# A decoder trunk on one core: squares summed by VectorE, the first expert's rows found by themselves, output weights in order of use

## What is computed

```python
for l in range(DEPTH):
    h = rms_norm(x, mix_norm[l])
    p = h @ w_in[l]
    y = concat([rwkv7_mix(p), short_conv_mix(p), dilated_attention_mix(p)])
    x = x + y @ w_o[l]
    h = rms_norm(x, ffn_norm[l])
    if l == 0: x = x + swiglu(h, dense_wg, dense_wu, dense_wd)
    else:
        topv, topi = top_k(h @ router, 2); gates = softmax(topv)
        x = x + sum of gates * swiglu(h, moe_wg[e], moe_wu[e], moe_wd[e]) over the chosen e
```

## Time and profile before

| | us |
|---|---|
| median of 3 runs | 1449.14 |
| the profiled execution, whole | 1449.35 |
| its span, first to last instruction | 1447.5 |
| mean granted TensorE clock | 0.992 of full speed |
| TensorE busy | 1424.3 (98%) |
| weight load busy | 1100.1 (76%) |
| VectorE busy | 870.2 (60%) |
| ScalarE busy | 722.9 (50%) |
| GpSimd busy | 72.5 (5%) |
| transfers | 440.84 MB, mean 305 GB/s |

### The profile page before, as it was taken

The page is one execution under the profiler, slowest core; times in us unless marked ns, Lnnn a source line. Parts: engine busy times, 40 slices in busy tenths (PEclk is TensorE's granted clock), DMA queues, the critical chain, the costliest instruction groups (busy, mean ns, idle before and its releaser), DMA issues.

```text
span 1447.5 us, 24888 instructions
## 1 busy us (share of the span) xinstructions
PE 1424.3 (98%) x10480; PEld 1100.1 (76%) x10480; DVE 870.2 (60%) x1136; ACT 722.9 (50%) x991; POOL 72.5 (5%) x61
## 2 busy tenths in 40 slices
PE   8999999999999999999999999999999999999997
PEld 8988999999999889733788634888535888888532
DVE  7587855555557887311899311999203999899300
ACT  6545544444455645200888302888103887888200
POOL 0004000010000050000000000000000000000000
PEclk9999999999999999899999999999999999999999
DMA  9600455554544400999999999999999999999996
GB/s 342 221 36 4 186 193 185 193 176 175 175 163 175 139 3 3 392 416 421 421 420 422 421 422 421 421 421 420 421 421 422 420 414 423 407 421 415 348 422 263
DMA packets 64838, 440.84 MB, mean 305 GB/s; under 512 B 8000, under 2 KB 10576, under 8 KB 12112
## 3 DMA queue, kind: packets, MB, share of 16 engines
q1 hardware_dynamic: 63344, 434.46, 74.4%
q0 software_dynamic: 960, 3.15, 1.4%
q10 hardware_dynamic: 416, 1.57, 0.3%
HBM read 434.96 MB, written 2.62 MB: 302 GB/s over the span
## 4 chain that ended last, share of the span: by engine, by line
PE 91%; DMA 5%; DVE 2%; ACT 1%; issue 0%; SPq 0%; POOL 0%; DVEq 0%; POOLq 0%; ACTq 0%
PE bank L893 20%; PE bank L895 19%; PE bank L894 19%; PE bank L874 12%; PE bank L1605 11%; PE bank L1623 5%; DMA arena<-in_moe_wu 5%; PE bank L1568 1%; PE bank L1613 1%; PE bank L1638 1%; DMA ring<-in_w_in 0%; PE bank L1067 0%; PE bank L914 0%; PE bank L1320 0%; PE bank L1642 0%
## 5 line engine op out<-in xcount | busy, mean ns | idle before, releaser
L1744 ACT ACTIVATE w_hi<-ring 128x1024 fp32r<-128x1024 f32 x284 | 298.7, 1060 | 175.1 <-PE bank L895 169.4
L893 PE MATMUL bank<-w_hi,acts_hi 128*128 128x512 f32 x672 | 265.1, 394 | 0.0
L895 PE MATMUL bank<-w_hi,acts_lo 128*128 128x512 f32 x672 | 261.8, 390 | 0.0
L894 PE MATMUL bank<-w_lo,acts_hi 128*128 128x512 f32 x672 | 261.7, 389 | 0.0
L893 PE MATMUL bank<-acts_hi,w_hi 128*128 128x256 f32 x796 | 227.2, 285 | 1.1 <-DVE acts_lo L2497 0.8
L894 PE MATMUL bank<-acts_lo,w_hi 128*128 128x256 f32 x796 | 225.2, 283 | 0.0
L895 PE MATMUL bank<-acts_hi,w_lo 128*128 128x256 f32 x796 | 225.2, 283 | 0.0
L2568 DVE TENSOR_TENSOR w_lo<-arena,w_hi 128x1024 fp32r<-128x1024 f32 x144 | 175.1, 1224 | 13.2 <-ACT w_hi L1744 7.4
L2568 DVE TENSOR_TENSOR w_lo<-ring,w_hi 128x1024 fp32r<-128x1024 f32 x144 | 174.7, 1224 | 13.5 <-ACT w_hi L1744 7.7
L2903 DVE TENSOR_TENSOR arena<-arena,bank 128x256 f32<-128x256 f32 x28 | 11.8, 422 | 271.2 <-ACT arena L2171 271.2
L1744 ACT ACTIVATE w_hi<-arena 128x1024 fp32r<-128x1024 f32 x144 | 152.8, 1065 | 37.2 <-PE bank L895 37.2
(11 more groups left out here) (309 smaller groups left out, 1935.8 us busy)
## 6 DMA issues: line engine op xcount, KB each, us to landing
ring<-in_moe_wu SPq DMA_DIRECT2D x56, 1024.0 KB, 22.0
ring<-in_moe_wg SPq DMA_DIRECT2D x56, 1024.0 KB, 22.0
arena<-in_moe_wd SPq DMA_DIRECT2D x56, 1024.0 KB, 23.3
arena<-in_moe_wu SPq DMA_DIRECT2D x52, 1024.0 KB, 22.2
arena<-in_moe_wg SPq DMA_DIRECT2D x36, 1024.0 KB, 22.1
ring<-in_moe_wd SPq DMA_DIRECT2D x32, 1024.0 KB, 20.3
ring<-in_w_in SPq DMA_DIRECT2D x24, 1024.0 KB, 7.1
late<-in_moe_wg SPq DMA_DIRECT2D x16, 1024.0 KB, 22.8
```

The lines of the kernel that those rows point to most:

```text
L893: pe.matmul(out_, a_hi, b_hi, start=first, stop=False, **kw)
L894: pe.matmul(out_, a_hi, b_lo, start=False, stop=False, **kw)
L895: return pe.matmul(out_, a_lo, b_hi, start=False, stop=final, **kw)
L1744: return act.activation(o, i, ACT.Copy, **kw)
```

## The change

- **Sums of squares.** VectorE adds the eight squared slices up in `hT` with four instructions (`add_squares`: three of 128x512, one of 128x256) ahead of its next weight splits. TensorE then multiplies only the sum, with two products of one column in place of sixteen. This is done for n = 1 and n = 2.
- **The first expert's rows.** Who belongs to expert 0 is found without the full routing: a token does if fewer than two logits exceed its own for expert 0. Three rank products follow, then the seats. The raw rows `x_tok`, not the normalised ones, are gathered by four products of 512 columns, and the seats' inverse roots by four of one column; ScalarE scales the rows, TensorE turns them, and VectorE multiplies by the gains into `xb`. The full routing and the normalised rows come after that on VectorE, and the full ranks on TensorE behind the first half of the first chunk. The products of `keep_awake` are five, one before and two, two, two, one after. ScalarE waits for the normalised rows before it copies the first chunk (both use `spare`).
- **Output weights.** `w_o` is laid out on the host in the order of use, so its pieces 0 to 3 come from the halves in places 0 and 1. The expert weights' ring order becomes `late`, 0, 1, 4, 5, 2, 3 and the rest, and each load waits for the last user of its own place.

```diff
-            for two in (1, 2, 3, 0):
-                seen = max(WO_ORDER.index(2 * two), WO_ORDER.index(2 * two + 1)) + 1
-                stream += [("o", l, two, 0, (lo_ready, WO0[l] + seen))]
+            stream += [("o", l, two, 0, (lo_ready, WO0[l] + 2 * two + 2)) for two in range(KT // 2)]
...
         LATE = DEEP - 2
-        ring_places = [LATE] + e_slot[:SLOTS] + [s for s in range(SLOTS, DEEP) if s != LATE]
+        SPLIT_EARLY = (0, 1)
+        ring_places = [LATE, *SPLIT_EARLY] + [s for s in e_slot[:SLOTS] if s not in SPLIT_EARLY]
+        ring_places += [s for s in range(SLOTS, DEEP) if s != LATE]
...
-                            sp.wait_ge(*stream[e_before[n - 1]][4])
+                            sp.wait_ge(*stream[user[p_slot[n]]][4])
...
-            def sum_squares(n, k):
-
-                pe.wait_ge(sq_ready, KT * (n - 1) + k + 1)
+            def sum_squares(n):
+                pe.wait_ge(sums_stepped, 4 * n)
                 for b in range(2):
-                    last = pe.matmul(bank[SUM_BANKS[n]][:, b:b + 1], hT[:, k, b * P:(b + 1) * P], ones[:, 0:1],
-                                     start=k == b == 0, stop=k == KT - 1, skip_group_check=True)
-                if k == KT - 1:
-                    last.then_inc(ss_ready, 1)
+                    last = pe.matmul(bank[SUM_BANKS[n]][:, b:b + 1], hT[:, 0, b * P:(b + 1) * P], ones[:, 0:1],
+                                     start=b == 0, stop=True, skip_group_check=True)
+                last.then_inc(ss_ready, 1)
...
-                    elif j >= 2:
-                        sum_squares(1, 2 * j - 4)
-                        sum_squares(1, 2 * j - 3)
                 if l:
                     turn_rows(3)
-                    keep_awake(7, 5)
+                    keep_awake(7, 2)
...
                             if kind == "g" and j == 0 and q == 1:
-                                for k in range(4, KT):
-                                    sum_squares(1, k)
+                                sum_squares(1)
...
-            sel = small[:, 0:16]
-            pe.wait_ge(route_sel, 1)
-            mm(bank[6][:, 0:8], const("tri"), sel[:, 0:8])
-            mm(bank[6][:, 8:16], const("tri"), sel[:, 8:16], True, False)
-            mm(bank[6][:, 8:16], ones, sel[:, 0:8], False, True)
-            mm(bank[6][:, 16:24], ones, sel[:, 0:8], True, False)
-            mm(bank[6][:, 16:24], ones, sel[:, 8:16], False, True).then_inc(rank_done, 1)
-            keep_awake(7, 1)
+            def first_ranks():
+                pe.wait_ge(route_sel, 1)
+                mm(bank[5][:, 0:1], const("tri"), first_sel[:, 0:1])
+                mm(bank[5][:, 1:2], const("tri"), first_sel[:, 1:2], True, False)
+                mm(bank[5][:, 1:2], ones, first_sel[:, 0:1], False, True).then_inc(rank_done, 1)
+            def gather_first():
+                pe.wait_ge(hot_ready, 1)
+                pe.wait_ge(act_turned, 4)
+                for b in range(2):
+                    for g in range(2):
+                        last_ = pe.matmul(bank[1][g * C:(g + 1) * C, :], hot[0][:, b, 0:C],
+                                          x_tok[:, b, g * CW:(g + 1) * CW], start=b == 0, stop=b == 1,
+                                          skip_group_check=True)
+                pe.wait_ge(ms_ready, 4)
+                for b in range(2):
+                    for g in range(2):
+                        last_ = pe.matmul(bank[5][g * C:(g + 1) * C, 2:3], hot[0][:, b, 0:C], rms[:, b:b + 1],
+                                          start=b == 0, stop=b == 1, skip_group_check=True)
+                last_.then_inc(ga_done, 1)
+                keep_awake(7, 2)
+                pe.wait_ge(rows_kept, 1)
+                for i in range(4):
+                    last_ = pe.transpose(bank[2][:, i * P:(i + 1) * P], first_rows[:, i * P:(i + 1) * P], ident)
+                last_.then_inc(rows_kept, 1)
+                keep_awake(7, 1)
+            def all_ranks():
+                sel = small[:, 0:16]
+                pe.wait_ge(route_sel, 2)
+                mm(bank[5][:, 8:16], const("tri"), sel[:, 0:8])
+                mm(bank[5][:, 16:24], const("tri"), sel[:, 8:16], True, False)
+                mm(bank[5][:, 16:24], ones, sel[:, 0:8], False, True)
+                mm(bank[5][:, 24:32], ones, sel[:, 0:8], True, False)
+                mm(bank[5][:, 24:32], ones, sel[:, 8:16], False, True).then_inc(rank_done, 1)
...
-            gather_half(1, hot[0], True)
+            first_ranks()
+            keep_awake(7, 2)
+            gather_first()
...
+                        if q == hf == 0:
+                            all_ranks()
...
+            def keep_first_rows():
+                act.wait_ge(ga_done, 1)
+                act.wait_ge(seat_ready, 1)
+                act.activation(first_rows, bank[1][:, :], ACT.Identity, scale=seat_rms).then_inc(rows_kept, 1)
...
-            begin(0)
+            act.wait_ge(ht_ready, 2)
...
+            def add_squares(n, i):
+                dve.wait_ge(sq_ready, KT * (n - 1) + min(2 * i + 2, KT))
+                if i > 1:
+                    dve.wait_ge(sums_stepped, 4 * (n - 1) + i - 1)
+                if i < KT // 2:
+                    TT(hT[:, 0:2, :], hT[:, 0:2, :], hT[:, 2 * i:2 * i + 2, :], ALU.add).then_inc(sums_stepped, 1)
+                else:
+                    TT(hT[:, 0, :], hT[:, 0, :], hT[:, 1, :], ALU.add).then_inc(sums_stepped, 1)
...
+                add_squares(2, 1)
                 dve.wait_ge(x_ffn, 4)
                 for k in (KT - 2, KT - 1):
                     scaled_low(k, u_hi, u_lo, k, param(1, "mix_norm", k), u_high, KT, u_low)
+                for i in range(2, 5):
+                    add_squares(2, i)
...
+                    add_squares(1, 1)
                     for k in (KT - 2, KT - 1):
                         scaled_low(k, h_hi, h_lo, DENSE_PLACE[k], param(0, "ffn_norm", k), h_high, KT, h_low)
+                    for i in range(2, 5):
+                        add_squares(1, i)
...
-            largest(top1, first)
-            then(STT(logits, first, -3e38, logits, ALU.mult, ALU.add))
-            largest(top2, second)
-            TT(sel, first, second, ALU.add).then_inc(route_sel, 1)
-            dve.wait_ge(row_squared, 4)
-            TT(rms, row_sums[:, 0:2], row_sums[:, 2:4], ALU.add).then_inc(ss_ready, 1)
-            then(TT(e2, top2, top1, ALU.subtract))
-            dve.wait_ge(rt_ready, 4)
-            then(dve.reciprocal(rms, rms))
-            TT(e2, e2, rms, ALU.mult).then_inc(route_act, 1)
+            def first_members():
+                then(TT(per(cand), per(logits), stretch(per(logits)[:, :, 0], NE), ALU.is_gt))
+                then(dve.tensor_reduce(at_, per(cand), AX.X, ALU.add))
+                TS(first_sel, at_, 1.5, None, ALU.is_lt).then_inc(route_sel, 1)
+            def first_places():
+                dve.wait_ge(rank_done, 1)
+                then(STT(rank_first, bank[5][:, 0:2], 1.0, first_sel, ALU.add, ALU.mult))
+                STT(hot[0][:, :, 0:C], spread(const("iota")[:, 0:C], 2), 1.0, stretch(rank_first, C), ALU.add,
+                    ALU.is_equal).then_inc(hot_ready, 1)
+            def first_tokens():
+                dve.wait_ge(rows_kept, 2)
+                gains_of = prm[:, N_PARAM * (L - 1) + PARAM_COLS["ffn_norm"][0]:][:, 0:KT]
+                TT(xb.rearrange("p (g i) t -> p i g t", g=2),
+                   bank[2][:, :].rearrange("p (i g t) -> p i g t", i=4, g=2),
+                   gains_of.rearrange("p (g i o) -> p i g o", g=2, o=1).to_broadcast([P, 4, 2, C]),
+                   ALU.mult).then_inc(ga_kept, 1)
...
+            first_members()
+            dve.wait_ge(sums_stepped, 8 + 4)
+            TT(rms, row_sums[:, 0:2], row_sums[:, 2:4], ALU.add).then_inc(ss_ready, 1)
+            first_places()
+            dve.wait_ge(rt_ready, 4)
+            dve.reciprocal(rms, rms).then_inc(ms_ready, 1)
+            largest(top1, first)
+            dve.wait_ge(ga_done, 1)
+            dve.tensor_copy(seat_rms, bank[5][:, 2:3]).then_inc(seat_ready, 1)
+            then(STT(logits, first, -3e38, logits, ALU.mult, ALU.add))
+            first_tokens()
+            largest(top2, second)
+            TT(sel, first, second, ALU.add).then_inc(route_sel, 1)
+            then(TT(e2, top2, top1, ALU.subtract))
+            TT(e2, e2, rms, ALU.mult).then_inc(route_act, 1)
             dve.wait_ge(gain_in, 16)
             normal_rows(0)
-            dve.wait_ge(rank_done, 1)
-            then(STT(rank_first, per(bank[6][:, 0:16])[:, :, 0], 1.0, per(sel)[:, :, 0], ALU.add, ALU.mult))
-            STT(hot[0][:, :, 0:C], spread(const("iota")[:, 0:C], 2), 1.0, stretch(rank_first, C), ALU.add,
-                ALU.is_equal).then_inc(hot_ready, 1)
-            TS(rank_sums, bank[6][:, 0:3 * NE], 1.0, None, ALU.mult)
             normal_rows(1)
```

(9 more changed lines are left out.)

25 lines of the change are left out of this document (14 added, 11 removed).

## The result

The changed kernel takes 1436.36 us (median of 4 runs, 1435.42 to 1437.15), the kernel before 1448.74 (median of 4). The ratio on record is 0.9909, with a 95% interval of 0.9895 to 0.9924: 12.4 us faster by the medians, 13.2 (11.0 to 15.2) by the ratio times 1449.14. The forecast was 11.15 us. In the profiled executions the whole went from 1449.35 to 1437.15 (12.2 us) and the span from 1447.5 to 1435.3.

The account below looks back on a forecast made before the run. The expert stage was taken as bound almost equally by weight transfers and TensorE. 1449.35 - 4.75 (norms) - 6.4 (expert stage) = 1438.2, against the median 1438.0; range 1436 to 1445.

Parts of the forecast that it names:

- part 1: Sums of squares in the two norms: 1.0 us won in layer 0, 3.75 in layer 1, 4.75 in all.
- part 3: First expert's rows, routing: TensorE's path 5.6 us earlier, full ranks later costing 1.1 us.
- part 2: Output weights in order of use: two halves fetched within the recurrence, 5.0 us of transfer moved out of the later stretch.
- The two bounds: Expert stage: TensorE and transfers bind almost equally; speeding up only one gains at most 1.4 us, so both must move.
- Rival C: Routing: clock falls earlier, or early halves are useless because TensorE alone is late; 1 to 1.5 us left, 1443.3; chance 0.10.
- The smaller of the two: Expert stage: TensorE's own way 7.0 us ahead, transfers 6.4; the smaller, 6.4, holds.
- D: Layer 1's norm: clock still falls, from the 0.9 us stall for the reciprocal; 1.7 us less, 1439.7; chance 0.08.
- H: Norms: VectorE's adds cost as much as was saved, and Rival C besides; about 1447.5, no visible change; chance 0.06.
- One sign that the forecast set itself: Either norm: the forecast is wrong if TensorE idles for VectorE longer than 0.9 us.
- The clock in the routing: New routing before the first expert: full clock assumed, narrowly, because wide products fill most of its 8 us.
- B: New routing: clock falls at about 602 as before; 4.0 us instead of 6.4, 1440.4; chance 0.20.
- F: TensorE at half clock from the logits on: stream 4.8 us later, layer 1's clock lost too; 1451; chance 0.05.

Follow-up runs that it names:

- e1: The changed kernel again, unaltered, beside the kernel before on the first chip: 1435.78 us, ratio 0.991.
- e12: The changed kernel again, unaltered, on the third chip: 1436.36 us, ratio 0.9915.
- e5: Changed kernel with VectorE's last three additions behind two weight splits and TensorE's sum and spread one piece later, both norms: 1434.81 us, ratio 0.9905.
- e11: Changed kernel with the last three additions behind two weight splits, run again beside the unaltered changed kernel on the third chip: 1434.72 us, ratio 0.9904.
- e2: Changed kernel with the sums of squares undone, TensorE again multiplying all eight squared slices: 1442.57 us, ratio 0.9959.
- e3: Changed kernel with the old ring order, so only one half is fetched early; w_o keeps its new layout: 1441.27 us, ratio 0.9949.
- e10: Kernel before with only the new first-expert routing and the new w_o layout; old ring order and old sums: 1448.29 us, ratio 0.9993.
- e7: Kernel before with four keep-awake products instead of one between the ranks and the gather: 1448.0 us, ratio 0.9984.
- e6: Changed kernel without the seven keep-awake products (two, two, two, one) in the routing: 1440.11 us, ratio 0.9939.
- e9: Kernel before with only the new sums of squares: 1443.82 us, ratio 0.9971.
- e8: Kernel before with only w_o in order of use and two more halves fetched in the recurrence: 1447.13 us, ratio 0.9988.
- e4: Changed kernel with the old full routing before the first expert; new sums and early halves stay: 1441.57 us, ratio 0.9949.

## Why the prediction was nearly right, and where it was not

All executions together give an account of the stage behind the mixers. G is what TensorE itself gained from the mixers' end to the end of its first 48 expert products (41.95 us in the kernel before: 608.36 + 12.55 - 578.96); W is its waits for transfers (1.4 before); A is what the last scatter gained behind the mixers. If nothing else plays a part, A = G + 1.4 - W. That sum is bookkeeping; it does not say which limit is the nearer. For that T is counted by itself, over the bytes landed: how much sooner behind the mixers' end than in the kernel before 200 MB of expert weights are there, the early halves included.

```text
kernel            mixers end    G      W     G+1.4-W     A      T
after               574.11     5.69   1.0     6.1      6.4    6.2
e1  (after)         573.48     5.69   1.8     5.3      5.4    6.0
e12 (after)         574.03     5.69   1.4     5.7      5.8    5.9
e5  later sums      571.09     5.67   1.3     5.8      5.9    6.0
e11 later sums      571.17     5.68   1.2     5.9      6.2    6.0
e2  no part 1       580.46     5.69   1.2     5.9      6.2    6.2
e3  no early        573.26     5.69   5.2     1.9      1.6    1.4
e10 part 3 alone    578.35     5.68   5.4     1.7      1.4    1.3
e7  before, awake   579.27     4.32   4.1     1.6      1.6    1.4
e6  no awake        573.26     2.69   0.4     3.7      4.1    4.0
e9  part 1 alone    573.76     1.62   1.8     1.2      1.4    1.1
e8  part 2 alone    580.41     0.02   1.2     0.2      0.2    0.1
e4  no part 3       571.92    -1.60   1.4    -1.6     -1.6   -1.5
```

- **The two bounds: shown.** G of 5.7 gives 1.4 to 1.6 without the early halves (e3, e10), the early halves give 0.2 without G (e8), both together 5.4 to 6.4. In every version A is T within 0.3 us (e1: 0.6), and T lies below TensorE's own G + 1.4: the transfers are the nearer limit throughout. TensorE sets T in its turn where the ring is full (e8, e4, e6), by when it frees a place. Even e9 follows: its G is 1.6, its A stops near the 1.4 us of standing which the forecast gave the transfers, and W rises. This is the step "both have to move". Rival C's half that the early halves are of no use falls with e3.
- **Part 3: right in its size.** TensorE's own way was forecast at 5.6 us and is 5.67 to 5.69 in every execution of the new routing with its keep-awake products. The ranks took 1.21 us (1.1 forecast). The steps before the stream: forecast 603.5 less 4.75 is 598.75, measured 598.49.
- **The smaller of the two: right within the spread, with the wrong remainder.** 6.4 was forecast; the six executions with all that bears on it give 5.4 to 6.4, mean 6.0. The forecast's own numbers leave 7.0 - 6.4 = 0.6 us of waits, and the text nevertheless said that they would be a little longer than 1.4: a slip of sign. Measured they are 1.0 to 1.8. The transfers' own advance explains most of that: 5.69 + 1.4 - 6.2 leaves 0.9 us in the kernel after, with 1.0 measured; 5.69 + 1.4 - 5.9 leaves 1.2 in e12, with 1.4 measured. T is 0.2 to 0.5 below the 6.4 because the transfers lose a little once more, where the forecast had them stand no longer: at 16 MB they are 6.3 to 6.4 us ahead in the three executions of the changed kernel, at 20 MB 6.0 to 6.2. In e8 and e4 the waits stay at 1.2 and 1.4 for the same reason: once the ring has been full the transfers are no further ahead than TensorE is.
- **Part 1, layer 1: right, 3.82 against 3.75**, the clock included: 17.54 us from the addition to the end of the spread, then 13.72. The additions took 0.69 and 0.43 us, nearly as put, but stand 0.80 apart because of the semaphore between them. Rivals D and H fall.
- **Part 1, layer 0: right, 1.11 against 1.0.** The same 16.93 to 16.94 us stand in all five profiled executions with the old sums (before, e2, e7, e8, e10) and 15.83 to 15.84 in after, e1, e3, e6, e9 and e12. One sign that the forecast set itself came, though: TensorE idled for VectorE for 0.47 + 0.53 + 0.35 = 1.35 us in this norm, with 0.9 as the mark. The forecast's own working has more (181.9 to 182.7 and 185.6 to 186.4), so it is the mark that contradicts the working; the mechanism stands.
- **The place of the additions costs 2.4 us**: from VectorE's first addition in layer 0 to the mixers' end it takes 400.3 us in e5 and e11, and 402.6 to 403.0 in the seven executions with the additions in front (after, e1, e3, e4, e6, e9, e12). The forecast saw the wait and took it as the price of the exchange; it did not ask which splits TensorE needs first.
- **The clock in the routing: stays full, as forecast**; rivals B and F fall. That it was narrow is shown by e6: without the seven keep-awake products it falls twice and costs 3 us of G. The Trainium skill (TensorE: Matmul & The Clock Gate, Part 4: PE-mode transpose) would have made the transposes the weak place. In e6 the first fall, at 592.9, comes 4.5 us before the four of the new routing (597.43), behind two waits for VectorE and one-column products, but also behind the eight of `turn_rows` (from 587.54 and 588.79); the second, at 599.7, comes behind the four. No run here tells whether the page's rule had a part in that.
- **Why the total is 1.2 us beyond the forecast, and the ratio just under the low end of 1436.0.** The two terms were right, 4.93 us in the norms (4.75 forecast) and 6.36 behind the mixers (6.4). The step that failed is the sum: 1449.35 - 4.75 - 6.4 rests on one execution of the kernel before and puts everything outside the two terms at nothing. The pair of profiled executions by stretches, in us won:

```text
stretch                                             forecast   measured
start to VectorE's first addition, layer 0            0         -0.50
from there to the end of layer 0's spread             1.0        1.11
layer 0's dense part                                  0          0.02
from the addition at its end to layer 1's spread      3.75       3.82
from there to the mixers' end                         0          0.40
mixers' end to the last scatter                       6.4        6.36
last scatter to the end of the span                   0          0.99
sum                                                  11.15      12.20
```

Three of the terms outside are draws of the execution. First, from the last scatter to the end of the span takes 6.2 us (after) to 7.2 us (before), with 6.3 to 7.0 in the twelve experiments and no order by kernel: the pair stands at both ends of it, 1.0 us. Second, the start: the first addition stands between 170.58 and 171.51 in thirteen of the profiled executions, and at 169.09 in e4, without its low clock at launch. Third, the low clock in layer 1: from the first addition to the mixers' end it takes 407.8 to 408.1 us with the old sums and 3.4 us of low clock (before, e7, e10), 409.7 with 6.8 us (e2, e8), and 402.6 to 403.0 with the new ones. So part 1 is worth 5.2 us in one execution and 6.9 in another, and the forecast took 4.75 for all. 5.2 to 6.9 and 6.0 together are 11.2 to 12.9; the medians gave 11.8 to 12.6.

Which of these moved the medians is not shown. The profiled execution of the kernel before, with one low stretch in layer 1, had the mean clock of the median run beside e1 (0.992), and e9's runs give part 1 alone no more than 4.2 us. The distance itself is within chance: the medians' 1436.36 lies inside the range of 1436 to 1445, the ratio times 1449.14 is 1435.95, and the forecast's 1438.0 is 0.9923 of 1449.14, inside the interval. Only the three gains together, all above 11.15, say that the forecast was low.

The runs of the kernel before show the low clock's part without a trace: beside e1 their times go with the mean granted clock, 1443.84 us at 0.996, 1446.15 at 0.994, 1448.33 at 0.992, 1452.08 at 0.990. That is 8.2 us for 0.006, 1.4 us for each 0.001, and 0.001 of 1448 us is what 2.9 us at half speed take away, worth 1.45 us. The changed kernel has 0.997 to 0.999 and a spread of 2.3 us. Part of its gain is that it no longer loses this time: 1.7 us for each low stretch in layer 1. In the routing the clock gave TensorE 4.3 us (e7), but alone only 1.6 of them came through behind the mixers, since the transfers bind there. The range had no room on the lower side for a draw of this kind. One more low stretch of 3.4 us in layer 1, as in two of the five executions with the old sums, is 1.7 us: it would have put the low end at 1434.3.

Not settled: why e11's median shows less than its last scatter, why the profiled execution of the changed kernel was each time its slowest, the 0.4 us between layer 1's norm and the mixers' end, what the transfers lose between 16 and 20 MB, and e1, where W is 0.7 us more than T explains.

## What to carry over

Where two limits stand almost equal, account for each separately from a common point (here the end of the mixers) and check that gain plus remaining waits add up; a part that gives nothing alone may be what pays out another. An execution's low-clock stretches are a draw, not a constant: before a trace is used as the base of a sum, set its granted clock beside that of the other runs, and give the range a term for one stretch more or less. An engine that takes over work should do it behind what the other engine waits for next, not in front.

## What was not expected of the hardware

- The clock falls with TensorE fully busy: in e2 it was busy 4.00 of 4.00 us from 426 to 430, fell at about 429.4 and ran at 0.50 from 430 to 435. The fall came within 32 one-column instructions, which took 4.13 us; in the profiled execution of before the same 32 took 3.63 us by the same view (3.46 in the chain of the earlier trace rows), and the clock fell at about 431.6, behind them. The Trainium skill (TensorE: Matmul & The Clock Gate, Part 1) explains falls by gaps between products; these rows show one without a gap, as far as modelled ends can tell.
- The same code had 3.4 us at the low clock in some executions and 6.8 in others (layer 1), 6.8, 10.2 or 13.7 in the old routing (e9, before, e4), and 3.4 or none at launch (e4).
- An addition of 128x512 that depends on the one ahead takes 0.69 us, like an independent operation of the shape (0.68), and one of 128x256 0.43. But the next one in the chain starts 0.80 us after it (180.73 and 181.53 in the chain of waits), while an operation that need not wait for it starts 0.60 us after (176.67 and 177.27).
